# Strassen block products for the gate and up projections of the four swiglu stages

## The reference

```python
def swiglu_ffn(x, wi, wo):                    # x 512 x 1024, wi 1024 x 5632, wo 2816 x 1024
    gate, up = jnp.split(x @ wi, 2, axis=-1)
    return (jax.nn.silu(gate) * up) @ wo

for l in range(2):
    x = layer_norm(alpha * x + 0.5 * swiglu_ffn(x, ffn1_wi[l], ffn1_wo[l]), ...)
    mix = even_mixer(x, ...) if l % 2 == 0 else odd_mixer(x, ...)
    x = layer_norm(alpha * x + mix, ...)
    x = layer_norm(alpha * x + 0.5 * swiglu_ffn(x, ffn2_wi[l], ffn2_wo[l]), ...)
```

## Time and profile before

| | |
|---|---|
| median of 3 runs | 3648.5 us (3648.3 to 3650.64) |
| profiled execution, span from the first to the last instruction | 3648.8 us |
| TensorE busy | 3572.4 us |
| DVE, ACT, POOL busy | 1675.8, 1344.7, 513.3 us |

### The profile page before, as it was taken

One profiled execution on the slowest core, in us unless ns is written; L12 is line 12 of the kernel. 1 busy time (PEld: TensorE's weight loads), 2 busy tenths in 40 slices (PEclk: granted clock), 3 DMA queues, 4 the chain that ended last, 5 costly groups with the idle time before them and its releaser, 6 DMA issues. The chain is left out here.

```text
span 3648.8 us, 47149 instructions
## 1 busy us (share of the span) xinstructions
PE 3572.4 (98%) x18876; PEld 2969.0 (81%) x18876; DVE 1675.8 (46%) x2195; ACT 1344.7 (37%) x1880; POOL 513.3 (14%) x483
## 2 busy tenths in 40 slices
PE   8999999999999999989999999999999999999998
PEld 7888876888888888778888887878888878888887
DVE  2223566322332235565422354656663536557643
ACT  3222544322232225453422242445442324454432
POOL 2102103210221021022210201011111001021110
PEclk9999999999999999999999999999999999999999
DMA  4222221222322222221222233222222333132222
GB/s 150 92 93 102 88 81 58 81 92 90 117 81 92 90 95 97 72 87 41 87 92 87 102 117 121 93 99 81 102 90 95 122 109 110 69 116 87 98 87 87
DMA packets 59663, 342.37 MB, mean 94 GB/s; under 512 B 7024, under 2 KB 10624, under 8 KB 31104
## 3 DMA queue, kind: packets, MB, share of 16 engines
q1 hardware_dynamic: 55552, 327.77, 25.2%
q0 software_dynamic: 3968, 12.59, 1.0%
HBM read 332.99 MB, written 7.34 MB: 93 GB/s over the span
## 5 line engine op out<-in xcount | busy, mean ns | idle before, releaser
L389 DVE TENSOR_TENSOR w_lo<-raw,w_hi 128x2048 fp32r<-128x2048 f32 (+2 forms) x305 | 642.7, 2107 | 809.5 <-ACT w_hi L384 793.9
L384 ACT ACTIVATE w_hi<-raw 128x2048 fp32r<-128x2048 f32 (+2 forms) x296 | 510.5, 1725 | 699.2 <-PE bank L427 596.2
L425 PE MATMUL bank<-x_hi,w_hi 128*128 128x512 f32 (+1 forms) x1920 | 746.5, 389 | 2.4 <-DVE w_lo L389 2.4
L426 PE MATMUL bank<-x_lo,w_hi 128*128 128x512 f32 (+1 forms) x1920 | 734.9, 383 | 0.0
L427 PE MATMUL bank<-x_hi,w_lo 128*128 128x512 f32 (+1 forms) x1920 | 734.8, 383 | 0.0
L425 PE MATMUL banks<-x_hi,w_hi 128*128 128x512 f32 (+1 forms) x1408 | 547.5, 389 | 17.5 <-POOL x_lo L623 10.2
L426 PE MATMUL banks<-x_lo,w_hi 128*128 128x512 f32 (+1 forms) x1408 | 542.1, 385 | 0.0
L427 PE MATMUL banks<-x_hi,w_lo 128*128 128x512 f32 (+1 forms) x1408 | 541.9, 385 | 0.0
L425 PEld LDWEIGHTS bank<-x_hi,w_hi 128*128 128x128 f32 x1920 | 361.5, 188 | 87.5 <-issue 15.4
L427 PEld LDWEIGHTS bank<-x_hi,w_lo 128*128 128x128 f32 x1920 | 361.6, 188 | 70.5
L426 PEld LDWEIGHTS bank<-x_lo,w_hi 128*128 128x128 f32 x1920 | 361.7, 188 | 70.3 <-issue 2.4
(11 more groups left out here) (529 smaller groups left out, 4550.0 us busy)
## 6 DMA issues: line engine op xcount, KB each, us to landing
raw<-in_weights SPq DMA_DIRECT2D x217, 1024.0 KB, 4.8
raw<-in_weights SPq DMA_DIRECT2D x96, 704.0 KB, 4.0
raw<-in_weights SPq DMA_DIRECT2D x8, 768.0 KB, 4.2
odd_arena<-in_kv SPq DMA_DIRECT2D x8, 512.0 KB, 3.6
x_kept<-X SPq DMA_DIRECT2D x2, 2048.0 KB, 12.8
X<-x_kept SPq DMA_DIRECT2D x2, 2048.0 KB, 10.8
work<-in_rpb POOLq DMA_DIRECT2D x12, 256.0 KB, 3.0
stats<-in_rpb POOLq DMA_DIRECT2D x12, 256.0 KB, 3.0
```

What stands on the lines that cost most here:

```text
L384: act.activation(w_hi[:, s, 0:size], raw[:, s, 0:size], ACT.Copy).then_inc(hi_ready.sem, 1)
L389: dve.tensor_tensor(w_lo[:, s, 0:size], raw[:, s, 0:size], w_hi[:, s, 0:size].bitcast(F32), ALU.subtract).then_inc(lo_ready.sem, 1)
L425: pe.matmul(out, wh[:, w], hi(k), start=first and n == 0, stop=False, skip_group_check=not group)
L426: pe.matmul(out, wh[:, w], lo(k), start=False, stop=False, skip_group_check=not group)
```

## The change

A chunk's weights are four blocks of 128x512, gate and up by the lower and the upper half of the input width. The activations are four blocks as well, halves of the width by halves of the tokens. From chunk 3 on (S0) the 2x2 product of blocks is made in the Winograd form of Strassen's method: seven block products (`block_product`) of 4 x 3 matmuls with 256 tokens, 84 in all, instead of 48 with 512. What this needs:

- **POOL** forms four sums and differences of the chunk's raw blocks, each 128x512 (`sums`), and keeps g's rest (`low_g`) only for chunks 0 to 9; for chunks 10 to 21 it is made at the end (`late_low`), and ACT rounds there too (`late_round`).
- **ACT** rounds seven blocks of 128x512 (`block_high`) instead of one of 128x2048, copies the first product out of PSUM (`copy_first`, 256 tokens), and takes the silu in two halves.
- **DVE** makes seven rests of 128x512 (`block_low`) and seven operations of 128x256 (`combine`: five additions and two products, six of them with one operand from PSUM, the last product with both in SBUF), instead of one rest of 128x2048 and one product of 128x512.
- **Activation combinations** T1 to T4 (128x1024 each) are made once a stage, in the place of X, and rounded and split on ACT, DVE and POOL. X is therefore stored to DRAM ahead of it (not in the first stage, whose input is there already) and loaded again when the last chunk's sixth block is done.

Products of one chunk go to four half banks, and two chunks alternate between two sets of them. Weight blocks 0 to 3 of every chunk have one place and blocks 4 to 6 another, so that block q of the next chunk can be rounded once block q of this chunk is used.

```diff
+S0, LATE = 3, 10
+own, other = n0 % 2, 1 - n0 % 2
...
+def weight_block(w, j, q):
+    at = q % 4 * 512
+    return w[:, other if q < 4 or isinstance(j, int) and j == FT - 1 else own, at:at + 512]
...
+def block_source(u, q):
+    return (raw_block(u, 2), sum_block(1), sum_block(2), sum_block(0), raw_block(u, 3), raw_block(u, 1),
+            sum_block(3))[q]
+T1R, T2R, T3R, T4R = X[:, 0:4, h1], X[:, 4:8, h1], block4(g_plain, 14), X[:, 4:8, h0]
+T_RAW = {1: T2R, 2: T3R, 3: T1R, 5: T4R}
+T_HIGH = {1: block4(g_hi, 10), 2: block4(g_hi, 12), 3: x_turned[:, 0:4, h0], 5: block4(g_hi, 16)}
...
+U1, U2, U3 = stats[:, 1, h0], stats[:, 0, h0], stats[:, 0, h1]
+REGIONS = (0, 1, 2, 3, 0, 2, 3)
+def region(u, r):
+    return bank[4 * (1 - u) + r][:, 0:HS]
...
+        if joined:
+            for t_ in range(2):
+                sp.wait_ge(rounded.sem, rounded.at((t_ + 1) * KT))
+                sp.dma_start(x_kept[:, :, halves[t_]], X[:, :, halves[t_]]).then_inc(x_stored.sem, 16)
+        with sp.Fori(1, FT // 2 - 1) as i:
+            for u in range(2):
+                first(i, u)
+        for u in range(2):
+            first(FT // 2 - 1, u)
+        second(0, 0)
+        sp.wait_ge(block_used.sem, used_of(FT - 1, 5))
+        sp.dma_start(X[:, :, :], x_kept if joined else t["x"]).then_inc(x_back.sem, 16)
+        second(0, 1)
...
+        def block_product(j, u, q):
+            if q == 6:
+                pe.wait_ge(lo_ready.sem, j + (PRIME + n0 + 1))
+            else:
+                pe.wait_ge(block_lo.sem, block_lo.at(-6 * S0 + q + 1) + j * 6)
+            if q == 0:
+                pe.wait_ge(product_ready.sem, product_ready.at(-1) + j)
+            elif q >= 4:
+                pe.wait_ge(combined.sem, combined_of(j, q - 3))
+            wh, wl = weight_block(w_hi, j, q), weight_block(w_lo, j, q)
+            out = region(u, REGIONS[q])
+            for k in range(4):
+                if q in T_RAW:
+                    xh, xl = T_HIGH[q][:, k, :], T_LOW[q][:, k, :]
+                else:
+                    kt, h = {0: (k, h0), 4: (4 + k, h0), 6: (4 + k, h1)}[q]
+                    xh, xl = x_hi[:, kt, h], x_lo[:, kt, h]
+                w = slice(k * P, k * P + P)
+                pe.matmul(out, wh[:, w], xh, start=k == 0 and q < 4, stop=False, skip_group_check=True)
+                pe.matmul(out, wh[:, w], xl, start=False, stop=False, skip_group_check=True)
+                mm = pe.matmul(out, wl[:, w], xh, start=False, stop=k == 3, skip_group_check=True)
+            mm.then_inc((chunk_used if q == 6 else block_used).sem, 1)
...
+        gate_up(1, 0)
+        blocks_of(S0, 1)
+        with pe.Fori(2, FT // 2 - 1) as i:
             for u in range(2):
-                gate_up(i, u)
+                blocks_of(i * 2 + u, u)
+        for j in (FT - 2, FT - 1):
+            blocks_of(j, j % 2)
+        pe.wait_ge(product_ready.sem, product_ready.at(FT - 1))
...
+        def block_high(j, u, q):
+            if q in (0, 4, 5):
+                act.wait_ge(raw_loaded[(n0 + u) % 2], half_loads(j, u))
+            else:
+                act.wait_ge(block_sums.sem, block_sums.at(-4 * S0 + (0, 2, 3, 1, 0, 0, 4)[q]) + j * 4)
+            if j is S0:
+                act.wait_ge(chunk_used.sem, PRIME + n0 + (2 if q < 4 else 3))
+            elif isinstance(j, int) and j == FT - 1 and q >= 4:
+                act.wait_ge(block_used.sem, used_of(j, q - 4))
+            elif q == 6:
+                act.wait_ge(chunk_used.sem, j + (PRIME + n0))
+            else:
+                act.wait_ge(block_used.sem, used_of(j - 1, q))
+            act.activation(weight_block(w_hi, j, q), block_source(u, q), ACT.Copy)\
+                .then_inc((hi_ready if q == 6 else block_hi).sem, 1)
...
+        def copy_first(j, u):
+            act.wait_ge(block_used.sem, used_of(j, 0))
+            act.activation(U1, region(u, 0), ACT.Copy).then_inc(first_copied.sem, 1)
...
+        def body(j, u, v, early):
+            block_high(j + 1, v, 0)
+            copy_first(j, u)
+            if early:
+                round_g(j - 1, v)
+            for q in (1, 2, 3):
+                block_high(j + 1, v, q)
+            half_silu(j, u, 1)
+            block_high(j + 1, v, 4)
+            block_high(j + 1, v, 5)
+            half_silu(j, u, 0)
+            block_high(j + 1, v, 6)
...
+        late_round(10)
+        late_round(11)
+        half_silu(FT - 1, 1, 1)
+        late_round(12)
+        late_round(13)
+        half_silu(FT - 1, 1, 0)
+        late_round(14)
+        split2(0, 0)
+        for j in range(15, FT):
+            late_round(j)
...
+        def block_low(j, u, q):
+            if q == 6:
+                dve.wait_ge(hi_ready.sem, j + (PRIME + n0 + 1))
+            else:
+                dve.wait_ge(block_hi.sem, block_hi.at(-6 * S0 + q + 1) + j * 6)
+            dve.tensor_tensor(weight_block(w_lo, j, q), block_source(u, q), weight_block(w_hi, j, q).bitcast(F32),
+                              ALU.subtract).then_inc((lo_ready if q == 6 else block_lo).sem, 1)
...
+        def combine(j, u, q, g):
+            if q == 1:
+                dve.wait_ge(block_used.sem, used_of(j, 1))
+                dve.wait_ge(first_copied.sem, first_copied.at(1 - S0) + j)
+                dve.tensor_tensor(U2, U1, region(u, 1), ALU.add).then_inc(combined.sem, 1)
+            elif q == 2:
+                dve.wait_ge(block_used.sem, used_of(j, 2))
+                dve.wait_ge(combined.sem, combined_of(j, 1))
+                dve.tensor_tensor(U3, U2, region(u, 2), ALU.add).then_inc(combined.sem, 1)
+            elif q == 3:
+                dve.wait_ge(block_used.sem, used_of(j, 3))
+                dve.wait_ge(combined.sem, combined_of(j, 2))
+                dve.tensor_tensor(silu[:, u, h1], U3, region(u, 3), ALU.add).then_inc(combined.sem, 1)
+            elif q == 5:
+                dve.wait_ge(block_used.sem, used_of(j, 5))
+                dve.tensor_tensor(silu[:, u, h0], U2, region(u, 2), ALU.add).then_inc(combined.sem, 1)
+            elif q == 6:
+                dve.wait_ge(chunk_used.sem, j + (PRIME + n0 + 1))
+                if g is None:
+                    dve.wait_ge(rest_ready.sem, rest_ready.at(-1) + j)
+                out = prod[:, u, :] if g is None else g
+                dve.tensor_tensor(out[:, h1], U2, region(u, 3), ALU.add).then_inc(combined.sem, 1)
+                dve.wait_ge(act_ready.sem, act_ready.at(1) + j)
+                dve.tensor_tensor(out[:, h0], silu[:, u, h0], region(u, 0), ALU.mult)
+                dve.wait_ge(combined.sem, combined_of(j, 5))
+                dve.tensor_tensor(out[:, h1], silu[:, u, h1], out[:, h1], ALU.mult).then_inc(product_ready.sem, 1)
...
+        def body(j, u, v, early):
+            g = None if early else g_plain[:, FT + j, :]
+            for q in range(7):
+                combine(j, u, q, g)
+                block_low(j + 1, v, q)
...
         if joined:
             lead_vector(dve, n0)
-            rest(0, 0)
-            rest(0, 1)
         else:
             whole_lead_vector(dve)
-            body(0, 0)
-            body(0, 1)
-        with dve.Fori(1, FT // 2 - 1) as i:
+            split(0, 0)
+            rest(0, 0)
+            split(0, 1)
+        dve.wait_ge(split_ready.sem, split_ready.at(lead_tiles))
+        dve.wait_ge(chunk_used.sem, PRIME + n0 + 2)
+        dve.tensor_tensor(T3R, T2R, T1R, ALU.subtract).then_inc(t_raw.sem, 1)
+        if joined:
+            rest(0, 0)
+        rest(0, 1)
+        if joined:
+            dve.wait_ge(x_stored.sem, x_stored.at(32))
+        dve.tensor_tensor(T1R, T1R, X[:, 0:4, h0], ALU.subtract).then_inc(t_raw.sem, 1)
+        dve.wait_ge(t_raw.sem, t_raw.at(2))
+        dve.tensor_tensor(T2R, T2R, T1R, ALU.subtract).then_inc(t_raw.sem, 1)
+        dve.wait_ge(t_raw.sem, t_raw.at(3))
+        dve.tensor_tensor(T4R, T4R, T2R, ALU.subtract).then_inc(t_raw.sem, 1)
+        block_low(S0, 1, 0)
+        t_split(2, 1)
+        block_low(S0, 1, 1)
+        t_split(1, 2)
+        block_low(S0, 1, 2)
...
+        def sums(j, u, ms):
+            a, s1, s2, s3, s4 = raw_block(u, 2), *(sum_block(m) for m in range(4))
+            for m in ms:
+                if m == 0:
+                    if isinstance(j, int):
+                        pool.wait_ge(raw_loaded[(n0 + u) % 2], ((n0 + j) // 2 + 1) * 16)
+                    else:
+                        pool.wait_ge(raw_loaded[(n0 + u) % 2], (j - u) * 8 + ((n0 + u) // 2 + 1) * 16)
+                    if j is S0:
+                        pool.wait_ge(chunk_used.sem, PRIME + n0 + 2)
+                    else:
+                        pool.wait_ge(block_lo.sem, block_lo.at(-6 * S0 + 4) + (j - 1) * 6)
+                    ins = pool.tensor_tensor(s1, raw_block(u, 0), raw_block(u, 1), ALU.add)
+                elif m == 1:
+                    pool.wait_ge(block_sums.sem, block_sums.at(-4 * S0 + 1) + j * 4)
+                    ins = pool.tensor_tensor(s2, s1, a, ALU.subtract)
```

(113 more changed lines are left out.)

122 lines of the change are left out of this document (98 added, 24 removed).

## The result

The changed kernel takes 3667.32 us (median, 3663.99 to 3669.06), the kernel before 3649.12 (3648.3 to 3650.64), four runs each: a ratio of 1.0044, 95% interval 1.0032 to 1.0057. It is slower by 0.4%. The forecast was 3612, faster by 1%, with 3594 to 3640 as its range. The profiled execution spans 3665.4 us, 16.6 more than before. Every ratio here is of fast runs: of the 17 executions of the three kernels under "Block products from chunk 5 on" four are left out as slow, at 4506 to 13140 us.

A forecast was written before the change was run, and what follows sets the result against it. TensorE, busy 3572.4 of 3648.8 us, was taken as the bound, so only fewer or shorter matmuls could gain in the gate/up part. 3648.8 - 60.8 + 7.8 + 8 + 6 + 2 = 3611.8; own range 3602 to 3628, with two rivals 3594 to 3640.

The forecast's parts named there:

- The matmuls: Chunks 3 to 21 of four stages: 84 matmuls 120.0 ns apart, 10.08 us a chunk instead of 10.88, gaining 60.8 us.
- The rival in which they cost 3650: TensorE's ten waits a chunk cost 0.05 us each, 38 us more, about no change; chance 0.05.
- POOL and DVE together: Early chunks: the two engines exclude each other, period 10.4 us against TensorE's 10.08; costs 8 us (0 to 20).
- Start of a joined stage: Chunk 2 waits for product 0 behind T3, 2.1 to 3.2 us in three stages: 7.8 us.
- First block chunk: Chunk 3: DVE reaches the rests of blocks 0 to 2 late, 1.5 us in each of four stages: 6 us (0 to 12).
- End of a stage: POOL's twelve g rests end behind the last matmul, 0.5 us a stage: 2 us (0 to 6).
- X back: Reload of X at a stage's end, 10.8 us, hidden behind two down chunks; without that cover up to 11 us a stage.
- The slower rival: POOL and DVE exclude each other for whole recorded durations, 11.8 us early and 10.5 late a chunk: 3670; chance 0.12.

The follow-up runs named there:

- Block products from chunk 5 on: Against the changed kernel, block products start at chunk 5 instead of 3: 0.9951 with product 0 ahead of T3, 0.9968 with T3 first, 0.9957 with eight filling matmuls.
- small sums: Changed kernel with POOL's four weight sums a chunk formed on 64 of 512 columns, output not the reference's: 0.9913 of the kernel before.
- the kernel with spread rests: Against chunk 5 on with products 0 and 2 first, POOL's g rests of chunks 5 to 9 made one per two late chunks: 0.9961, 3637.11 us.
- a T of 16 columns: Changed kernel with T1 to T4 and their splits formed on 16 of each 256 columns, output not the reference's: 0.9931 of the kernel before.
- from chunk 5 on with products 0 and 2 first: Against chunk 5 on with product 0 first, DVE also does product 2 and the split of chunk 4 ahead of T splits: 0.9939, 3629.98 us.
- the kernel from chunk 5 on with T3 first: Against chunk 5 on with product 0 first, T3 stands ahead of product 0 again: 0.9968 of the kernel before.

## Why the prediction was wrong, by its own steps

**The matmuls: right.** 120 ns a start, late chunks at 10.12 us. The waits on TensorE are free: 0.04 us a chunk over 84 x 0.12 leaves nothing for ten waits, and with small sums a chunk takes 10.08 with the same ten. The rival in which they cost 3650 is out.

**POOL and DVE together: the mechanism right, the size too small.** Forecast period 10.4, within 10.1 to 10.9; measured 10.6 to 10.8, but for the two chunks behind chunk 3 in the joined stages, with 10.1 to 10.3. The holds were right: in the late part of the kernel with spread rests two contended rests of DVE start at 754.95 and 756.66 and the next instruction at 758.36, 1.70 us each, beside POOL's (756.15, 757.85), and 1.16 + 0.533 is 1.69. Five of the one and seven of the other make 9.8 us of exclusive time, as forecast. What is left to 10.7, the time in which neither holds the ports, was put too small: 0.9 us, not 0.6. One further part of it is DVE's 0.40 us a chunk for ACT's rounding of block 5, which I had left out. And I let 1.5 us of slack absorb the lateness once, though `combine` is late in nearly each early chunk: 15.5 / 4 = 3.9 us a stage, not 2.

**Start of a joined stage: the wait right, the clock wrong.** 2.23 us was forecast as 2.1 to 3.2. "The granted clock should not fall in gaps of this size" is wrong: it fell to the 1.2 GHz level after each of the three, 1.6 us more. The lead's gaps, from which I argued, are shorter. It isn't a fixed price of such a gap, as the kernels from chunk 5 on show.

**First block chunk: this is the step that failed.** It was forecast at 6 us (0 to 12) and measured at 35. In a joined stage my date for block 2's rest, 679 to 681, looks right against the 680.8 measured, but only because the part ahead of this stage was faster: DVE began T3 at 661.00, not at 662.7. Counted from there, DVE was to reach block 2's rest after 16.3 to 18.3 us. It began it after 16.9, and ended it after 19.8, for the rest stood 2.84 us beside POOL's split of a T, which I had not charged to it. So I took 1.5 us for what is 2.4 at block 2, and had nothing for 2.5 more at block 4, where `combine` 1 stands behind three rests of chunk 3 and one of chunk 4. I had costed the way to block 2 and not looked at what DVE's order puts ahead of the first combine. In the first stage block 2 waits 4.5 us, since the need comes earlier by the whole of the missing gap. In this kernel the clock also fell behind these waits, which the forecast put at nothing: of the 8.0 us that chunk 3 is too long in the second stage 4.9 are waits, and the other 3.1 are for the most part 30 matmuls that start 213 ns apart instead of 120. The experiments show that it is work and not order: moving product 0 or the combines moves the wait, a T of 16 columns removes it but for 0.7 us in the first stage, two chunks more of time remove most of it.

**End of a stage: mis-sized.** 1.84 us a stage against 0.5: three gaps of 0.45, and the rest in pieces of 0.12 and less behind and ahead of them.

**X back: right**, no wait.

**The slower rival** gave 3670, near the measured time, for a reason that doesn't hold. It needs a mean cycle of 10.67 us; the measured mean of chunks 4 to 21 is 10.32, with 10.6 to 10.8 in the early ones where that rival has 11.8, and 10.12 in the late ones where it has 10.5. That 3670 comes near is luck. The Trainium skill (SBUF — State Buffer, Who interferes with whom) has the lock on the shared port pair, and the trace agrees on who takes part; the pair of 1.70 us shows that what is held is shorter than the two recorded durations, 1.30 and 0.69.

**What stays open.** Why the instructions outside the stages, which didn't change, take 4.7 us more. By the granted clock of the two traces, TensorE is at the lower level for 48 us before, all of it outside the four stages, and for 95 us after, 58 of them outside. Half of the 10 us more is about what is looked for, and stretch by stretch the times follow it. Between the first two stages the time at the lower level falls from 17 to 7 us, and the stretch gets 5.3 us shorter. Between the last two it rises from 24 to 31, and the stretch gets 4.7 longer. Behind the fourth it rises from 7 to 20, for 5.3 more. Most of TensorE's idle times there have the same lengths in both traces. Why the clock falls behind some of them in one trace and not in the other, no run here tells.

The best version that keeps the result, from chunk 5 on with products 0 and 2 first, beats both kernels: 0.9939 of the kernel before. Its 68 block chunks are worth 54 us by matmuls, and it keeps 20.

## What to carry to other kernels

When work is moved to an engine that shares ports with another, add the two up as one resource, and do that for the first pass through the loop by itself: the set-up and the loop's own run-ahead fall on the same few microseconds there. In such a pass, write down for each wait of the bottleneck engine what its releaser has queued ahead of it. A removed wait counts only if the chain behind it isn't late already; and an instruction taken from a full stretch has to go to one with room, or its cost goes with it.

## What the runs showed of the hardware

- An idle time of 2.23 us on TensorE, after dense work, was followed in the changed kernel each of three times by about six matmuls at full clock and then eight at 427 ns instead of 227, 1.6 us. In the kernel from chunk 5 on with T3 first, three gaps of the same length in the same places had no such fall (granted clock 1.00).
- A DVE instruction with two SBUF operands issued just after a POOL instruction of 128x1024 is recorded as busy for as long as it waits: 2.84 us for a rest of 0.69. A busy share of 96% on DVE (20.64 of 21.45 us) was about two thirds work, at the 6.5 us a chunk counted for it.
- DVE and POOL at 128x512 in turn go round in 1.70 us, less than the sum of their recorded durations, 1.99.
